# A chunked recurrence whose block inverse is turned by VectorE instead of TensorE

## The reference

```python
def step(s, inp):
    r_t, w_t, k_t, v_t, a_t, b_t = inp
    sa = jnp.einsum('bhvk,bhk->bhv', s, a_t)
    s = s * w_t[:, :, None, :] + sa[..., None] * b_t[:, :, None, :] + v_t[..., None] * k_t[:, :, None, :]
    y = jnp.einsum('bhvk,bhk->bhv', s, r_t) if emit else None
    return s, y
s_fin, ys = lax.scan(step, s0, xs, reverse=reverse)
```

## Time and profile before

| | |
|---|---|
| time, median of 3 runs | 2892.42 us (2891.69 to 2894.26) |
| profiled execution, first to last instruction | 2891.8 us |
| median of the runs less that span | 0.6 us |
| TensorE busy | 2785.9 us (96%), 29030 matmul records |
| VectorE busy | 1191.4 us (41%), 2524 instructions |
| ScalarE busy | 685.4 us (24%), 1425 instructions |
| granted TensorE clock, mean | 0.991 |
| recurrence of layer 0, whole chunks | about 172 to 345 us |
| recurrence of layer 1, whole chunks | about 1435 to 1606 us |

### The profile page before, as it was taken

The page is one execution under the profiler, slowest core; times in us unless marked ns, Lnnn a source line. Parts: engine busy times, 40 slices in busy tenths (PEclk is TensorE's granted clock), DMA queues, the critical chain, the costliest instruction groups (busy, mean ns, idle before and its releaser), DMA issues.

```text
span 2891.8 us, 63838 instructions
## 1 busy us (share of the span) xinstructions
PE 2785.9 (96%) x29030; PEld 1672.3 (58%) x29030; DVE 1191.4 (41%) x2524; ACT 685.4 (24%) x1425; POOL 3.0 (0%) x7
## 2 busy tenths in 40 slices
PE   7999999999999999999998999989999999999997
PEld 4467777445777888864577787863333333333332
DVE  4777565444546444237786564431111011011101
ACT  2345312544322111013454126520000000000000
POOL 0000000000000000000000000000000000000000
PEclk9999999999999999999999999999999999999999
DMA  7100143212232433232000442459999999999995
GB/s 293 59 3 4 47 148 122 66 44 84 91 127 78 146 117 90 80 120 84 30 4 5 168 160 96 148 218 348 413 364 365 415 359 378 400 364 412 364 379 199
DMA packets 188786, 534.55 MB, mean 185 GB/s; under 512 B 6112, under 2 KB 80096, under 8 KB 171104
## 3 DMA queue, kind: packets, MB, share of 16 engines
q1 hardware_dynamic: 187440, 526.21, 48.5%
q0 software_dynamic: 1072, 4.19, 0.4%
HBM read 528.29 MB, written 2.10 MB: 183 GB/s over the span
## 4 chain that ended last, share of the span: by engine, by line
PE 92%; DVE 3%; ACT 2%; issue 1%; SPq 1%; DMA 0%; DVEq 0%; ACTq 0%
PE bank L583 68%; PE bank L711 12%; PE bank L1357 8%; PE bank L829 2%; PE bank L1219 1%; SPq L3014 1%; ACT WR L1647 1%; DMA rep<-in_repeated 0%; ACT ar L1647 0%; PE bank L948 0%; DVE WR L2480 0%; DVE RS L2351 0%; PE bank L1519 0%; DVE ar L2410 0%; ACT L1647 0%
## 5 line engine op out<-in xcount | busy, mean ns | idle before, releaser
L583 PE MATMUL bank<-AT,WR 128*128 128x512 f32 (+1 forms) x1408 | 519.9, 519 | 6.3 <-ACT AT L1647 3.7
L1647 ACT ACTIVATE ar<-bank 128x256 f32<-128x256 f32 (+2 forms) x338 | 155.1, 463 | 1533.4 <-PE bank L583 1026.5
L583 PE MATMUL bank<-WR,ar 128*32 128x512 f32 (+1 forms) x4464 | 444.5, 555 | 1.6 <-DVE ar L2923 1.6
L583 PE MATMUL bank<-ar 128*32 128x512 f32 (+6 forms) x3990 | 429.6, 509 | 9.7 <-ACT ar L1647 5.7
L583 PEld LDWEIGHTS bank<-AT,WR 128*128 128x128 f32 x1408 | 262.4, 191 | 212.5 <-issue 196.4
L583 PEld LDWEIGHTS bank<-ar 128*32 128x32 f32 (+3 forms) x3990 | 176.1, 124 | 248.3 <-issue 236.4
L583 PEld LDWEIGHTS bank<-WR,ar 128*32 128x32 f32 x4464 | 143.7, 110 | 288.4 <-issue 285.8
L1647 ACT ACTIVATE WR<-bank 128x512 f32<-128x512 f32 (+1 forms) x224 | 125.1, 593 | 200.2 <-PE bank L583 166.7
L583 PE MATMUL bank<-AT,ar 128*32 128x512 f32 (+1 forms) x1456 | 151.4, 561 | 11.9 <-ACT AT L1647 11.9
L2933 DVE TENSOR_TENSOR YB<-YB,bank 128x512 f32<-128x512 f32 x28 | 18.0, 684 | 343.3 <-PE bank L583 343.3
L2941 DVE TENSOR_TENSOR ar<-ar,bank 128x512 f32<-128x512 f32 (+1 forms) x48 | 29.8, 621 | 286.5 <-PE bank L583 285.1
(11 more groups left out here) (368 smaller groups left out, 3296.6 us busy)
## 6 DMA issues: line engine op xcount, KB each, us to landing
WR<-in_moe_w_down SPq DMA_DIRECT2D x27, 2048.0 KB, 15.2
WR<-in_ada_w SPq DMA_DIRECT2D x20, 2048.0 KB, 8.2
ar<-in_moe_w_down SPq DMA_DIRECT2D x20, 2048.0 KB, 14.7
WR<-in_w_in SPq DMA_DIRECT2D x18, 2048.0 KB, 8.9
WR<-in_moe_w_gate SPq DMA_DIRECT2D x18, 2048.0 KB, 17.0
WR<-in_moe_w_up SPq DMA_DIRECT2D x15, 2048.0 KB, 16.2
WR<-in_moe_w_up SPq DMA_DIRECT2D x18, 1536.0 KB, 7.8
WR<-in_moe_w_gate SPq DMA_DIRECT2D x15, 1536.0 KB, 9.1
```

The source lines that it names most:

```text
L583: return pe.matmul(o, lhsT, rhs, start=first, stop=last)
L1647: return act.activation(out, in_, func, **k)
```

## The change

The products that made `XT` at levels 0 to 3 are gone. VectorE makes it instead from the copied `X[1]` with one transposing instruction, 128x512, that turns each block of 32 by 32 in its place (new function `turned`). That is the whole turned matrix as long as `X` is block diagonal in blocks of 32, so at levels 0 to 3. At level 4 the turned inverse is still made by TensorE and copied by ScalarE. ScalarE's four copies of `XT` per chunk at levels 0 to 3 go too.

With it the halves are laid out in another way: the Gram products and the turned values are written crosswise, and the products of `level` and of `inverse_doubled` are straight at all levels. `level_banks`, `grown_bank` and `turned_bank` now depend on the chunk alone.

```diff
         def level_banks(i, n):
-            return [banks[(0, 1, 6)[(5 * i + n + m) % 3]] for m in range(2)]
-        def grown_bank(i, n):
-            return banks[(0, 1, 6)[(5 * i + n + 2) % 3]]
-        def turned_bank(i, n):
-            return banks[(0, 1, 6)[(5 * i + n) % 3]]
+            return [banks[6 * (i % 2)], banks[1]]
+        def grown_bank(i):
+            return banks[6 - 6 * (i % 2)]
+        def turned_bank(i):
+            return banks[6 * (i % 2)]
...
                 def gram(i, what, bank, q, h):
                     ba, aa = BK[i % 2][64 * h:64 * h + 64, q, 0:64], pair(MV[:, i % 2, 0, :], q, h)
-                    return mm(pair(bank, q, h), *((aa, ba) if what == "X" else (ba, aa)), True, True)
+                    return mm(pair(bank, q, 1 - h), *((aa, ba) if what == "X" else (ba, aa)), True, True)
...
-                            ins = mm(pair(bank, q, 1 - h if n else h), pair(LTs[i % 2], q, h), pair(X[n > 0], q, h), True, True)
+                            ins = mm(pair(bank, q, 1 - h), pair(LTs[i % 2], q, 1 - h), pair(X[n > 0], q, 1 - h), True, True)
...
                 def inverse_doubled(i, n):
-                    x, t1 = (swapped(XT[1]), swapped(T1)) if n else (compact(XT[0]), compact(T1))
+                    x, t1 = swapped(XT[n > 0]), swapped(T1)
                     if n:
-                        pe.wait_ge(A.free, A.jobs[("XT", l, i, n - 1)])
-                    elif i:
+                        pe.wait_ge(turned_ready, seen(turned_ready))
+                    elif n == 0 and i:
                         pe.wait_ge(A.free, A.jobs[("XT", l, i - 1, 4)])
-                    if n < 4:
-                        A.done(("X", l, i, n))
-                    A.done(("XT", l, i, n))
+                    A.done(("X" if n < 4 else "XT", l, i, n))
                     for q in range(8):
                         if q % 4 == 0:
                             pe.wait_ge(S.free, S.jobs[("T1", l, i, n, q // 4)])
-                        if n < 4:
-                            for h in range(2):
-                                ins = mm(pair(grown_bank(i, n), q, h), x(q, h), t1(q, h), True, True)
-                                if (q, h) == (7, 1):
-                                    ins.then_inc(A.full, 1)
                         for h in range(2):
-                            last = mm(pair(turned_bank(i, n), q, 1 - h), t1(q, h), x(q, h), True, True)
+                            if n < 4:
+                                last = mm(pair(grown_bank(i), q, 1 - h), x(q, h), t1(q, h), True, True)
+                            else:
+                                last = mm(pair(turned_bank(i), q, 1 - h), t1(q, h), x(q, h), True, True)
                     last.then_inc(A.full, 1)
...
+                def turned(i, n):
+                    dve.wait_ge(A.free, A.jobs[("X", l, i, n)])
+                    dve.transpose(XT[1], X[1]).then_inc(turned_ready, 1)
...
                             rates_in(l, i + 1)
+                        turned(i, 0)
+                        if i < NCH - 1:
                             operands(l, i + 1)
                         masked(i, 1)
...
                             responses(l, i + 1)
+                        turned(i, 1)
                         state(i - 1)
...
                     kept(i, 0, 2)
+                    turned(i, 2)
                     if i + 2 < NCH:
                         centre(l, i + 2)
...
                     kept(i, 4, 6)
+                    turned(i, 3)
                     if i < NCH - 1:
                         begin_inverse(i + 1)
```

More of the change, by code:

```diff
@@ L446, in trunk @@
         inverse_ready, state_ready = sem("inverse_begun"), sem("state_ready")
+        turned_ready = sem("inverse_turned")
         bonus_ready = sem("bonus_ready")
@@ L831, in narrow @@
                 return last
-            def compact(x):
-                return lambda q, h: pair(x, q, h)
             def swapped(x):
@@ L858, in value_turned @@
                     c = CH * (i if q < 4 else BWD[i])
-                    last = mm(pair(gram_bank, q, h), Rv[64 * h:64 * h + 64, q % 4, c:c + CH],
+                    last = mm(pair(gram_bank, q, 1 - h), Rv[64 * h:64 * h + 64, q % 4, c:c + CH],
                               eye[64 * h:64 * h + 64, 64 * h:64 * h + 64], True, True)
@@ L937, in from_state @@
                 def from_state(i):
-                    right = grown_bank(i, 4)
+                    right = grown_bank(i)
                     bank = None
@@ L942, in from_state @@
                         bank = y_bank(i)
-                    pe.wait_ge(A.free, A.jobs[("XT", l, i, 3)])
+                    pe.wait_ge(A.free, A.jobs[("X", l, i, 3)])
                     if i:
@@ L1777, in recurrence @@
                         if n == 2:
-                            stacked_in(slice(64, 128), gram_bank, 0)
+                            stacked_in(slice(64, 128), gram_bank, 1)
                         if n < 4:
-                            copied(X[1], grown_bank(i, n))
+                            copied(X[1], grown_bank(i))
                         else:
-                            copied(G, grown_bank(i, n))
-                        copied(XT[1 + n // 4], turned_bank(i, n))
+                            copied(G, grown_bank(i))
+                            copied(XT[2], turned_bank(i))
                         if n in (2, 3) and i + 2 < NCH:
@@ L2526, in recurrence @@
                 operands(l, 1)
+                turned(0, 0)
                 shifted(l, 10)
@@ L2529, in recurrence @@
                 responses(l, 1)
+                turned(0, 1)
                 shifted(l, 11)
```

## The result

| | before | after |
|---|---|---|
| time, median | 2893.34 us (2891.69 to 2898.59, 4 runs) | 2923.39 us (2921.95 to 2925.25, 4 runs) |
| ratio to before | | 1.010, interval 1.0086 to 1.0114 |
| profiled execution, first to last instruction | 2891.8 us | 2923.5 us |
| granted clock, mean | 0.991 | 0.989 |

The changed kernel is 1.0% slower: 30.0 us by the medians, 31.7 by the profiled executions. The forecast was 2917 us, 2900 to 2938, slower with 0.85.

The account below looks back on a forecast made before the run. TensorE's waits bounded the kernel before; the change closes a ring through VectorE's in-order queue. Stages sum to 176.6 us per layer, 353.2 against 328.7: 24.5 more, 2916.3 span, plus 0.6: 2917 us, range 2900 to 2938.

Parts of the forecast that it names:

- The 0.6 us from the span to the time: Whole kernel: the runs' median lies 0.6 us above the profiled span, so 2916.3 becomes 2917 us.
- Half the products cost as long: TensorE's doublings: 32 records last 1.15 us like 64; removal returns only code waits, at most about 12.7 us plus small groups.
- ScalarE's copies give nothing: ScalarE: four copies per chunk go, about 0.5 us each, but they follow the awaited copy of X, so no gain.
- The transposing at 0.68 us: VectorE: each 128x512 transposing takes 681 ns, 0.59 to the next start; 58 of 64 stand on the path.
- 0 to 1 and 1 to 2: Between X copies of these levels: 4.81 us, then 4.52 late or 5.12 early; 33.7 and 33.3 us per layer.
- 2 to 3: From level 2's copy of X to level 3's: 4.44 us, 5.62 in early chunks; 39.1 us per layer.
- 3 to the next 0: From level 3's copy of X to the next chunk's level 0 copy: 9.73 to 10.1 us; 69.3 per layer.
- The 1.37 for the Gram read: Before level 4: begin_inverse stands behind level 3's transposing, so level 4 starts 1.37 us later.
- The clock: Rival: TensorE's clock falls to 1.2 GHz once per chunk, adding 22 us; 2932 to 2950 us, chance 0.13.
- Rival: only the Gram bank: Other VectorE work finds room elsewhere; only the later level 4 costs, 19.2 us less 12.7 to 19; around 2896, chance 0.08.
- Rival: code arrival: Late code bounds the kernel throughout; 14 to 16 fewer packets save 55 to 62 us, about 2834; chance 0.09 with milder form.
- Its milder form: VectorE keeps ahead and only the quoted waits for code go: 2880 us, within the 0.09 for 2834 to 2885.

Follow-up runs that it names:

- before_plus_turning: The kernel before with VectorE's transposings added at the changed kernel's places, written where nothing reads, and nothing taken away: 2926.48 us, 1.0132 to before.
- turn3_late: The changed kernel with level 3's transposing moved behind begin_inverse and the last two kept: 2907.20 us, 1.0050 to before.
- all_late: The changed kernel with all four transposings per chunk moved as late as they can stand in VectorE's order: 2883.16 us, 0.9961 to before.
- extra_cross: The changed kernel with the 16 turned products of levels 0 to 3 put back crosswise, their result unread: 2927.70 us, 1.0116 to before.
- extra_straight: The changed kernel with 16 more products at each of levels 0 to 3, placed straight, their result unread: 2976.42 us, 1.0301 to before.
- turned_twice: The changed kernel with each transposing issued twice, the first into a tile nobody reads: 2975.62 us, 1.0279 to before.
- before_shifted: The kernel before, TensorE's turned products kept, with bonus_keys at the chunk's end and all bonus work three chunks later: 2890.12 us, 0.9997 to before.

## Why the prediction was right

The time lies 6 us above the forecast, inside the range. The recurrences grew by 33.8 us and the first started 1.8 earlier, which leaves the span's 31.7 within 0.3; the forecast had 24.5. The 9.3 us that it is short in the recurrences are the clock above all (item 7), and the earlier start, which the forecast didn't have, hid a part of them: that much was luck. The 0.6 us from the span to the time was wrong too: each run lasts 1.7 to 2.1 us longer than its own span. The reason is the forecast's: before_plus_turning has the changed kernel's loss without its removals, and turn3_late and all_late take the loss away by the order alone.

1. *Half the products cost as long.* Right: 1.15 us for 32 records. extra_cross and extra_straight price the same products at 4 us, not told apart from nothing, and at 53. That removing them gives back waits for code wasn't so in the changed kernel: those waits fell by 9.6 us, but they are as short in extra_cross and in before_plus_turning, which have all the products.
2. *ScalarE's copies give nothing.* Right, as far as it shows: before_plus_turning keeps them and has the same floors.
3. *The transposing at 0.68 us.* I read it off transposings outside the recurrences. It takes 0.71, and 0.63 to the next start where I had 0.59.
4. *0 to 1 and 1 to 2.* Right within 0.1 and 0.2 us per layer, in part because errors cancel. From 0 to 1 the operands took 1.77 us (293.00 to 294.77) where I had 1.90, and from the first mask to the doubling it was 0.56 (294.77 to 295.33) where I had 0.47.
5. *2 to 3.* Mis-sized by 0.15 us per chunk. From the first mask's start to the doubling's I had 0.42 + 0.05, and it is 0.61 (303.80 to 304.41, where products of `against` also stand ahead of it). At level 1 to 2 the same was about 0.1 too short and hidden by the state's operations, 1.50 us (297.78 to 299.28) where I had 1.61. It makes 1.1 us per layer, 2.2 in both.
6. *3 to the next 0.* The 1.37 for the Gram read was exact as the distance of the floors, and 1.0 on the average of all 14 stages. The base was not: 8.36 was the shortest that I had quoted, and it still held 0.32 us of waiting; without any it is 8.04 (turn3_late). I then added 0.4 for code on top. Without the falls of the clock this stage came to 3.1 us less than forecast, both layers together.
7. *The clock.* A rival with 0.13, and I left it out of the sum. It fell in four places, and the stages hit are 10.0 us over their floors, at most 8.5 of them by the clock, where that rival had 22. The sum of the recurrences is forecast 350.8, + 2.2 (5) - 3.1 (6) + 10.0 (7) + 0.2 (4) = 360.1. It closes because each term is what was left of its stage, so it is no test. What I gave as its first reason, that doublings fill half as many places, is wrong (extra_cross). Its second, the new gaps, is right in kind, but not for the gaps that I named. I had them before each level 4. There TensorE waits for 1.3 us, and no fall follows; turn3_late takes these waits away and still has 6.8 us at 0.50. The falls follow the waits of 1.8 us for `kept` from 2 to 3, which I had not seen. In turned_twice, where both are longer (2.4 and 1.9), there are 44 us at 0.50; in all_late, whose longest wait is 1.6, none in the chunks. Why the same waits bring 17.0 us in one kernel, 27.2 in another and 6.8 in before_plus_turning isn't settled.
   The Trainium skill, page TensorE: Matmul & The Clock Gate, Part 1, says that the clock follows how busy the engine has been; the three stretches ahead of a fall, busy for 1.57, 1.58 and 1.60 of 3.40 us, agree, though the same wait of 1.8 us in another chunk often has no fall behind it.
8. *Rival: only the Gram bank.* Wrong as the whole; turn3_late measures that part at 16.2 us, with the falls of the clock that it spared, and 24.0 more went with the other three.
9. *Rival: code arrival.* Its strong form (2834) is refuted by the changed kernel and by all_late. Its milder form, in which VectorE keeps ahead and only the waits for code go, said 2880, and all_late comes near it with 2883.2: there these waits fell by 8.0 us. The changed kernel's order couldn't reach it.

## What to carry to other kernels

When an operation that waits for a late input is put into an in-order queue, set it behind all the work that is already due, as close as possible ahead of its reader: here the same four instructions per chunk cost 30 us in one set of places and win about 10 in another. Count small products by the busiest place of the array, not by their number: here products in an idle place cost next to nothing, and so little is won by removing them, unless TensorE is waiting for their code. Take a base for a term from the shortest of many stages, and ask of it too what it still waits for.

## What the runs showed of the hardware that was not expected

- 16 products of 64x64x64 in float32 cost 0.93 us more where they queue behind others in the same two places, and 0.03 to 0.04 us where they go to two idle places (extra_straight and extra_cross, by the floors).
- Code: 251 of TensorE's records (matmuls and weight loads) to a packet in the kernels with 231 and with 215 packets. Each wait for "issue" in the recurrences ends 1.2 to 1.6 us after such a packet has landed. In before_shifted the recurrences are 6.5 us shorter in one profile and the time isn't told apart, so these waits may mask what a reordering is worth.
- The transposing of 128x512 float32 takes 0.71 us between other operations of VectorE and 0.67 right behind another transposing.
- 3.4 us at clock 0.50 made a stage of 5.77 us 1.1 to 1.3 us longer (turn3_late 6.91 and 6.94, before_plus_turning 7.09). All but one of the falls in the recurrences of all these kernels come in or right after a single wait of TensorE of 1.7 to 2.4 us; many such waits have none behind them. Between kernels with the same floors the time at 0.50 differs from 6.8 to 27.2 us.
